# Dividing the eight PSUM banks of a recurrent mixer's loop anew: two pairs, one single bank, two for the attention

## The chip, the cores and the metric

The kernel runs on one core of one Trainium2 chip. The time is the device time of one execution in microseconds (us), from the hardware; lower is better. TensorE (PE) writes its matmul products to PSUM, which has eight banks; VectorE (DVE) and ScalarE (ACT) read them from there ("evict" them), GpSimd (POOL) works in SBUF, and SyncE (SP) issues most of the DMAs.

## The reference, cut to what matters

The program is two transformer blocks on a sequence of 1024 tokens with 1024 features. The second block mixes the tokens in two ways, and these two run together in the loop that is changed here:

```
y_fox  = fox_attention(q, k, v, log_f)                 # 8 heads of 64, causal, a decay as bias
for t in tokens:                                       # rwkv7_scan, 8 heads, state 64 x 64 a head
    sa = st @ a_t
    st = st * w_t + sa * b_t + v_t * k_t
    y_t = st @ r_t
merged = gate_fox * (y_fox @ w_o_fox) + gate_rwkv * (y_rwkv @ w_o_rwkv)
x      = x + merged @ w_out
```

The recurrent part ("rw" below) is computed in chunks: a triangular system is solved for each chunk of 64 tokens by doubling blocks, and only the state goes from chunk to chunk.

## The kernel before

The rw part is cut into eight units of 128 tokens (two chunks `c`, eight heads `h`). The function `b2` builds the loop. In each of its ten turns `together` interleaves three streams for every engine: `scan` of unit i-2, `inner` of unit i-1 and `pre` of unit i, and puts a piece of the attention ("fox", a `side` stream) between them. Each engine's order is fixed when the program is built, and an engine runs its instructions strictly in that order: a matmul that waits holds up everything behind it in PE's queue.

Every product takes a bank with `bk.take(key, ring)`. The ring is a tuple of bank numbers that are used in turn. The first matmul of the product waits until the bank's last product is evicted (`bk.room`, a semaphore `bank_emptied0` to `bank_emptied7`), its last matmul raises `bank_filled`, and DVE or ACT evict the bank and raise `bank_emptied`. A pair is named by its first bank and uses that bank's semaphores for both: pair 0 is banks 0 and 1.

These are the products of a unit, in PE's order around one turn of the loop, with the line of their matmuls and of the eviction:

- single products (`ONE_BANK`): `rw_n` (3596), `rw_b` (3601, evicted by DVE 3643), four turned operands `rw_turn` 0 to 3 (3608; 0 and 2 evicted by ACT 3697, 1 and 3 by DVE 3655), `rw_u` (3556, ACT 3872), `rw_k` 0 and 1 (3921 and 3922, DVE 3968), `rw_o` 0 and 1 (3931, DVE 3971), `rw_g` and `rw_kv` (both 3771, ACT 3862 and 3867), `rw_ot` (3940) and `rw_gate` (3950, DVE 3994);
- products of two banks (`PAIR`): `rw_mb` and `rw_qb` (both 3569, DVE 3823 and 3825, 3833 and 3834), `rw_t` (3758 and 3761, DVE 3839 and 3840), five times `rw_y` (3783, DVE 3845) and `rw_x` (3793 and 3797, DVE 3850 and 3854), `rw_w` (3812, ACT 3874), `rw_a` 0 and 1 (3906, DVE 3963 and 3964);
- the attention (`FB`): scores `fx_s` (3156), turned weights `fx_t` (3168), norms `fx_n` (3276), `fx_yt` (3288); its sums `fx_y` (3180) have bank 7 (`YB`).

The attention's first part runs earlier, between the matmuls of the gate projection (`a4`), which use banks 0 to 3. After the loop `pe_tail` begins the output projection: four tiles `o_tiles[:4]` of `w_o_fox` (lines 719 to 721, `pe_first_steps`) whose banks it is given as a ring. Then come a barrier and phase `a5`, whose first four tiles, of `w_o_rwkv`, take banks 0 to 3 of the common ring and wait for the room of all four before their first matmul. DVE evicts all these tiles at line 4115.

Of the kernel before, what the change touches and what calls it, by code (L numbers as in the profile page):

```python
# [218 lines left out]
def rest(n):  # L219
    for _ in range(n):  # L220
        yield
# [22 lines left out]
def program(nc, D, out, S):  # L244
# [3 lines left out]
    with ExitStack() as ctx:  # L248
        sigs = []

        def sem(name):
            return ctx.enter_context(nc.semaphore(name))
# [4 lines left out]
        def sig(name, step=1):  # L257
            n, of = over[step].pop() if over[step] else (0, sem(name))
            sigs.append(Sig(of, step))
            sigs[-1].n = sigs[-1].base = sigs[-1].covered = n  # L260
            return sigs[-1]
# [36 lines left out]
        def R(off, n, p0=0, p1=128):  # L298
            if off < H0:
                return XR[p0:p1, off:off + n]  # L300
            return BF[p0:p1, off - H0:off - H0 + n]
# [35 lines left out]
        bk = Banks(PS, [sem(f"bank_filled{b}") for b in range(8)], [sem(f"bank_emptied{b}") for b in range(8)])  # L337
# [10 lines left out]
        lhi, llo = sig("part_high"), sig("part_low")  # L348
# [37 lines left out]
        def nth(j):  # L386
            return sum(i not in by_blocks for i in range(j + 1))
# [4 lines left out]
        def wview(t, j):  # L392
            nk, n = order[j][2], order[j][4]
            return t[j % 2][:, 0:nk * n].rearrange("p (k c) -> p k c", k=nk)
# [309 lines left out]
        def pe_first_steps(e, tiles, x, ready, feats=None, side=None, at=None, ring=None):  # L704

            j, nk = tiles[0].j, tiles[0].nk
            wh, wl = wview(WH, j), wview(WL, j)
            ps = [bk.take(t.key, ring or RING) for t in tiles]
            e.wait_ge(s_wlo, nth(j))
            for t in tiles:  # L710
                e.wait_ge(*bk.room(t.key))
            for i, k in enumerate(feats or range(nk)):
                if i == at:
                    side(e)
                e.wait_ge(*ready(i))
                xh, xl = x(k)
                for n, t in enumerate(tiles):
                    sl, c = slice(t.hf * 512, t.hf * 512 + 512), slice(t.b, t.b + 128)
                    e.matmul(ps[n], wh[:, k, c], xh[:, sl], start=(i == 0), stop=False)  # L719
                    e.matmul(ps[n], wl[:, k, c], xh[:, sl], start=False, stop=False)  # L720
                    m = e.matmul(ps[n], wh[:, k, c], xl[:, sl], start=False, stop=(i == nk - 1))
                    if i == nk - 1:
                        m.then_inc(*bk.fill(t.key))
                yield
            wend[j] = bk.filled(tiles[-1].key)
# [2373 lines left out]
        def b2():  # L3099
# [4 lines left out]
                assert at_[0] <= F0 + 10 * T  # L3104
                return at_[0] - n

            PAIR, ONE_BANK, FB, YB = (0,), (2, 3), (4, 5, 6), (7,)
            QF, KF, VF, NCB = X0, X0 + T, X0 + 2 * T, [X0 + 3 * T, X0 + 4 * T]

            yo, free = R(F0 + 10 * T + 6, 512), F0 + 10 * T + 518  # L3110
# [319 lines left out]

            def pe_tail(e):
                yield from rest(TAIL + 2)
                yield from pe_first_steps(e, o_tiles[:4], hp, llo.at, None, None, None, (4, 5, 6, 7))

            def ve_tail(e):
                yield from rest(TAIL + 1)
# [37 lines left out]
            o_tiles = out_tiles()  # L3474
# [413 lines left out]
            def pe_scan(e, i):  # L3888
                u, w, rt, bb, kb, vT = (x[i % 2] for x in (us, wTs, rts, bbs, kbs, vTs))
                for b in range(2):  # L3890
                    h = (64 * b, 64 * b + 64)
                    key = ("rw_a", i, b)
                    bk.take(key, PAIR)
                    ps = bk.pair(key)
                    if b == 0:
                        e.wait_ge(*bk.emptied(("rw_w", i)))
                    if i + b == 0:
                        e.wait_ge(*rw_zero.at(0))
                    if i or b:
                        e.wait_ge(*bk.emptied(("rw_k", *divmod(2 * i + b - 1, 2))))  # L3900
                    e.wait_ge(*bk.room(key))
                    for at in (0, 256):
                        for q in range(4):
                            for g in range(2):
                                s_ = (64, 64 * g, 64 * g + 64)
                                m = e.matmul(ps[h[0]:h[1], g, at + 64 * q:at + 64 * q + 64],
                                             R(rt + q * 128 + 64 * b, *s_) if at else R(w + 256 * b + 64 * q, *s_),
                                             SR[64 * g:64 * g + 64, 64 * q:64 * q + 64], start=True, stop=True)
                    m.then_inc(*bk.fill(key))
                    yield  # L3910
                    key = ("rw_k", i, b)
                    ps = bk.take(key, ONE_BANK)
                    if b == 0:
                        for n in (2, 3):
                            e.wait_ge(*bk.emptied(("rw_turn", i, n)))
                    e.wait_ge(*rw_sub.at(2 * i + b))
                    e.wait_ge(*bk.room(key))
                    for q in range(4):
                        for g in range(2):
                            o, s_ = ps[64 * g:64 * g + 64, 64 * q:64 * q + 64], (64, *h)  # L3920
                            e.matmul(o, R(kb + (2 * q + g) * 64, *s_), R(vT + (2 * q + g) * 64, *s_), start=True, stop=False)
                            m = e.matmul(o, R(bb + (2 * q + g) * 64, *s_), R(u + (4 * g + q) * 64, *s_), start=False, stop=True)
                    m.then_inc(*bk.fill(key))
                    key = ("rw_o", i, b)
                    ps = bk.take(key, ONE_BANK)
                    if b == 0:
                        e.wait_ge(*bk.emptied(("rw_qb", i)))
                    e.wait_ge(*bk.room(key))
                    for q in range(4):
                        for g in range(2):  # L3930
                            m = e.matmul(ps[h[0]:h[1], (2 * q + g) * 64:(2 * q + g) * 64 + 64],
                                         R(qbs[i % 2] + (4 * g + q) * 64, 64, *h), R(u + (4 * g + q) * 64, 64, *h), start=True, stop=True)
                    m.then_inc(*bk.fill(key))
                    yield
# [130 lines left out]
        def out_tiles():  # L4065
            tiles = []
            for f in range(0, 8, 2):
                js = [wtile(n, 0, 4, f * 128, 256) for n in ("w_o_fox_2", "w_o_rwkv_2")]
                for s, j in enumerate(js):
                    for ff in range(2):  # L4070
                        for hf in range(2):
                            tiles.append(Tile(("o", s, f + ff, hf), j, 4, ff * 128, 128, 512, f + ff, hf, s,
                                              ff + hf == 0, ff + hf == 2))
            return tiles

        o_tiles = b2()
# [357 lines left out]
```

## Time and profile before

| | |
|---|---|
| time, median of 3 runs | 4202.17 us (4191.96 to 4206.91) |
| time of the profiled execution | 4194.41 us, span 4193.1 us |
| the recurrent loop | from about 2611 to 3150 us of the span |
| PE busy in 2631 to 3145 us | 403.85 of 514 us, granted clock 0.80 |
| DVE, ACT, POOL busy there | 283.30, 171.05, 124.87 us |

Most of the 4193 us are dense matmul phases outside the loop. In the loop no engine is always busy. "Granted clock" is the share of TensorE's full speed that the chip gave.

### The profile page before, as it was taken

The page shows a single profiled execution, that of the slowest core. Times are in us where ns is not written, and L with a number is a line of the kernel's source. Part 1 is how long each engine was busy: PE and PEld are TensorE (multiplying, and loading weights), DVE is VectorE, ACT ScalarE, POOL GpSimd, SP SyncE. Part 2 cuts the span into 40 slices and gives each one's busy share as a digit, 9 for nine tenths or more (in the row PEclk, how much of TensorE's full clock was granted, in tenths as well). Part 3 has the DMA queues.
Part 4 walks back from the last instruction along what each step waited for, and adds up shares of the span by engine and source line. Part 5 has one row for each costly group of instructions (what it writes and reads, how often), then busy time and mean ns, then how long its engine had stood idle before and what let it go on. Part 6 is the DMA issues. An engine that isn't in the chain of part 4 may idle for free. (4 is left out here: it accounts for less than half of the span.)

```text
span 4193.1 us, 75887 instructions
## 1 busy us (share of the span) xinstructions
PE 3875.4 (92%) x33370; PEld 3177.0 (76%) x33370; DVE 2251.9 (54%) x3662; ACT 1196.0 (29%) x1700; POOL 446.9 (11%) x440
## 2 busy tenths in 40 slices
PE   6999969888999999999999898788878999999999
PEld 5888847777867888888798576566667888888877
DVE  4643335555434666666624333555644476676673
ACT  5221234433223433121400323323323311111132
POOL 0001103231000442000000001222212000000000
PEclk9999979997999999999999899877879999999999
DMA  5211120113112334322322422111004211111111
GB/s 182 84 59 48 63 96 6 33 33 135 41 72 80 101 118 159 129 97 83 111 86 96 135 74 79 56 36 46 22 29 163 91 50 41 51 51 41 51 46 66
DMA packets 228061, 318.71 MB, mean 76 GB/s; under 512 B 17149, under 2 KB 172541, under 8 KB 227605
## 3 DMA queue, kind: packets, MB, share of 16 engines
q1 hardware_dynamic: 199088, 251.13, 18.1%
q10 hardware_dynamic: 28644, 62.72, 3.9%
q8 instruction: 265, 4.34, 0.4%
q14 instruction: 64, 0.52, 0.0%
HBM read 235.46 MB, written 78.35 MB: 75 GB/s over the span
## 5 line engine op out<-in xcount | busy, mean ns | idle before, releaser
L469 PE MATMUL ps<-sb_a_h,sb_whi 128*128 128x512 f32 (+1 forms) x2336 | 932.0, 399 | 6.2 <-DVE sb_wlo L430 5.7
L471 PE MATMUL ps<-sb_a_h,sb_whi 128*128 128x512 f32 (+1 forms) x2336 | 914.9, 392 | 0.0
L470 PE MATMUL ps<-sb_a_h,sb_wlo 128*128 128x512 f32 (+1 forms) x2336 | 914.8, 392 | 0.0
L469 PEld LDWEIGHTS ps<-sb_a_h,sb_whi 128*128 128x128 f32 (+1 forms) x2336 | 441.3, 189 | 116.6 <-issue 16.1
L470 PEld LDWEIGHTS ps<-sb_a_h,sb_wlo 128*128 128x128 f32 (+1 forms) x2336 | 441.6, 189 | 95.0 <-issue 5.2
L471 PEld LDWEIGHTS ps<-sb_a_h,sb_whi 128*128 128x128 f32 (+1 forms) x2336 | 440.9, 189 | 94.9
L420 ACT ACTIVATE sb_whi<-sb_wraw 128x2048 fp32r<-128x2048 f32 (+3 forms) x132 | 233.7, 1771 | 810.4 <-PE ps L471 494.5
L675 DVE TENSOR_TENSOR sb_x<-sb_x,ps 128x512 f32<-128x512 f32 x480 | 314.7, 683 | 211.5 <-PE ps L471 197.1
L430 DVE TENSOR_TENSOR sb_wlo<-sb_wraw,sb_whi 128x2048 fp32r<-128x2048 f32 (+3 forms) x132 | 281.9, 2135 | 224.6 <-ACT sb_whi L420 203.9
L469 PE MATMUL ps<-sb_a_g,sb_whi 128*128 128x512 f32 x896 | 349.8, 390 | 11.5 <-DVE sb_x L675 10.5
L471 PE MATMUL ps<-sb_a_g,sb_whi 128*128 128x512 f32 x896 | 348.7, 389 | 0.0
L470 PE MATMUL ps<-sb_a_g,sb_wlo 128*128 128x512 f32 x896 | 348.6, 389 | 0.0
L469 PEld LDWEIGHTS ps<-sb_a_g,sb_whi 128*128 128x128 f32 x896 | 168.2, 188 | 50.6 <-DVE sb_x L675 14.7
L471 PEld LDWEIGHTS ps<-sb_a_g,sb_whi 128*128 128x128 f32 x896 | 168.2, 188 | 35.1
L470 PEld LDWEIGHTS ps<-sb_a_g,sb_wlo 128*128 128x128 f32 x896 | 168.2, 188 | 34.6
L4230 DVE TENSOR_TENSOR sb_a_f<-ps,sb_root 128x512 f32<-128x512 f32 x88 | 60.9, 692 | 101.9 <-PE ps L471 96.2
L3249 POOL TENSOR_TENSOR sb_b<-sb_x,sb_consts 128x128 f32<-128x128 f32 x64 | 30.1, 485 | 611.0 <-DMA sb_x<-fox_c 399.2
L4280 ACT ACTIVATE sb_a_g<-sb_a_f 128x512 fp32r<-128x512 f32 x44 | 27.8, 633 | 226.0 <-DVE sb_a_f L4250 226.0
L526 PE MATMUL ps<-sb_a_h,sb_whi_blocks 128*128 128x512 f32 x224 | 87.2, 389 | 0.0
L527 PE MATMUL ps<-sb_a_h,sb_wlo_blocks 128*128 128x512 f32 x224 | 87.2, 389 | 0.0
L528 PE MATMUL ps<-sb_a_h,sb_whi_blocks 128*128 128x512 f32 x224 | 87.2, 389 | 0.0
L719 PE MATMUL ps<-sb_a_h,sb_whi 128*128 128x512 f32 x128 | 56.5, 442 | 25.0 <-DVE sb_wlo L430 8.5
(589 smaller groups left out, 6657.9 us busy)
## 6 DMA issues: line engine op xcount, KB each, us to landing
sb_wraw<-w_in SPq DMA_DIRECT2D x33, 1024.0 KB, 5.2
sb_wraw<-w_ff SPq DMA_DIRECT2D x32, 1024.0 KB, 5.4
sb_wraw<-w_up SPq DMA_DIRECT2D x22, 1024.0 KB, 5.1
sb_wraw<-w_down SPq DMA_DIRECT2D x11, 1024.0 KB, 4.9
sb_wraw<-w_xkv SPq DMA_DIRECT2D x8, 1024.0 KB, 5.5
sb_wraw<-w_out SPq DMA_DIRECT2D x8, 1024.0 KB, 5.3
sb_b<-rw_d SPq DMA_DIRECT2D x16, 512.0 KB, 6.4
sb_b<-y SPq DMA_DIRECT2D x16, 512.0 KB, 5.8
```

The costliest lines, as they stand in the source:

```text
L420: e.activation(WH[j % 2][:, 0:m], WR[j % 2][:, 0:m], ACT.Copy).then_inc(s_whi, 1)
L430: e.tensor_tensor(WL[j % 2][:, 0:m], WR[j % 2][:, 0:m], WH[j % 2][:, 0:m].bitcast(F32), ALU.subtract).then_inc(s_wlo, 1)
L469: e.matmul(o, wh[:, k, c], xh[:, sl], start=(k == 0), stop=False)
L470: e.matmul(o, wl[:, k, c], xh[:, sl], start=False, stop=False)
L471: m = e.matmul(o, wh[:, k, c], xl[:, sl], start=False, stop=(k == t.nk - 1))
L526: e.matmul(o, wh[:, k, :], xhi, start=(opens and k == 0), stop=False, skip_group_check=True)
L527: e.matmul(o, wl[:, k, :], xhi, start=False, stop=False, skip_group_check=True)
L528: m = e.matmul(o, wh[:, k, :], xlo, start=False, stop=(k == 3), skip_group_check=True)
L675: e.tensor_tensor(o, o, bk[t.key], ALU.add).then_inc(*bk.empty(t.key))
L719: e.matmul(ps[n], wh[:, k, c], xh[:, sl], start=(i == 0), stop=False)
L3249: e.tensor_tensor(nms[g], R(NCB[g] + qb * 128, 128), C("causal"), ALU.subtract).then_inc(*fx_nm[g].up())
L4230: e.tensor_tensor(raw[:, 2:514], bk[t.key], RR[:, span(t.hf)], ALU.mult).then_inc(*bk.empty(t.key))
```

## The change

The change deals the eight banks of `b2` out anew. Pair products get two pairs in turn, 0 and 1 or 2 and 3, except the last unit's two `rw_a`, which use only pair 0. Single products, which had banks 2 and 3 in turn, have bank 4 alone. The attention has banks 5 and 6 where it had 4, 5 and 6, in the part between the gate matmuls too. The four tiles of `pe_tail` use banks 2, 3, 5 and 6 where they used 4 to 7.

```diff
@@ -3104,7 +3104,7 @@
-            PAIR, ONE_BANK, FB, YB = (0,), (2, 3), (4, 5, 6), (7,)
+            PAIR, LAST_PAIR, ONE_BANK, FB, YB = (0, 2), (0,), (4,), (5, 6), (7,)
@@ -3430,7 +3430,7 @@
             def pe_tail(e):
                 yield from rest(TAIL + 2)
-                yield from pe_first_steps(e, o_tiles[:4], hp, llo.at, None, None, None, (4, 5, 6, 7))
+                yield from pe_first_steps(e, o_tiles[:4], hp, llo.at, None, None, None, (2, 3, 5, 6))
@@ -3890,7 +3890,7 @@
                 for b in range(2):
                     h = (64 * b, 64 * b + 64)
                     key = ("rw_a", i, b)
-                    bk.take(key, PAIR)
+                    bk.take(key, PAIR if i < 7 else LAST_PAIR)
                     ps = bk.pair(key)
```

No instruction is added, removed or moved on any engine; only addresses in PSUM and what is waited for change. On PE, where `rw_turn` 0 and 1 of unit 1, the last `rw_x` of unit 0, `rw_turn` 2 and 3 of unit 1 and `rw_u` of unit 0 follow each other, before:

```order
L3608 MATMUL ps<-sb_consts,sb_b 128x128 [waits bank_emptied2,rw_al]
...
L3608 MATMUL ps<-sb_consts,sb_b 128x128 [waits bank_emptied3,gd_in1]
...
L3793 MATMUL ps<-sb_b 64x32 [waits bank_emptied0]
...
L3608 MATMUL ps<-sb_consts,sb_b 128x128 [waits bank_emptied2,rw_k_end]
...
L3608 MATMUL ps<-sb_consts,sb_b 128x128 [waits bank_emptied3,rw_b_end]
...
L3556 MATMUL ps<-sb_b 64x64 [waits bank_emptied2,bank_emptied0]
```

and after:

```order
L3608 MATMUL ps<-sb_consts,sb_b 128x128 [waits bank_emptied4,rw_al]
...
L3608 MATMUL ps<-sb_consts,sb_b 128x128 [waits bank_emptied4,gd_in1]
...
L3793 MATMUL ps<-sb_b 64x32 [waits bank_emptied0,bank_emptied2]
...
L3608 MATMUL ps<-sb_consts,sb_b 128x128 [waits bank_emptied4,rw_k_end]
...
L3608 MATMUL ps<-sb_consts,sb_b 128x128 [waits bank_emptied4,rw_b_end]
...
L3556 MATMUL ps<-sb_b 64x64 [waits bank_emptied4,bank_emptied0]
```

Each of the four turned operands and `rw_u` now wait for the eviction of the single product just ahead of them; before they waited for the one before that.

On PE a little later, where `rw_mb` of unit 1 follows the first `rw_a` of unit 0, and then `rw_k`, `rw_o`, `rw_qb`, the second `rw_a`, `rw_t`, `rw_g`, `rw_k`, `rw_o` and `rw_kv`, before:

```order
L3569 MATMUL ps<-sb_b 64x64 [waits rw_kt,bank_emptied0,rw_bt,rw_al]
...
L3921 MATMUL ps<-sb_b 64x64 [waits rw_u_more,bank_emptied3,bank_emptied2]
...
L3931 MATMUL ps<-sb_b 64x64 [waits bank_emptied2,bank_emptied0]
...
L3569 MATMUL ps<-sb_b 64x64 [waits bank_emptied0,rw_rt]
...
L3906 MATMUL ps<-sb_b 64x64 [waits bank_emptied0,bank_emptied3]
...
L3758 MATMUL ps<-sb_consts,sb_b 64x64 [waits bank_emptied0,rw_x0]
...
L3771 MATMUL ps<-sb_b 64x64 [waits bank_emptied3,bank_emptied0]
...
L3921 MATMUL ps<-sb_b 64x64 [waits bank_emptied2,rw_u_more]
...
L3931 MATMUL ps<-sb_b 64x64 [waits bank_emptied3]
...
L3771 MATMUL ps<-sb_b 64x64 [waits bank_emptied2,bank_emptied3,bank_emptied0]
```

and after:

```order
L3569 MATMUL ps<-sb_b 64x64 [waits rw_kt,bank_emptied2,rw_bt,rw_al]
...
L3921 MATMUL ps<-sb_b 64x64 [waits rw_u_more,bank_emptied4]
...
L3931 MATMUL ps<-sb_b 64x64 [waits bank_emptied4,bank_emptied2]
...
L3569 MATMUL ps<-sb_b 64x64 [waits bank_emptied0,rw_rt]
...
L3906 MATMUL ps<-sb_b 64x64 [waits bank_emptied2,bank_emptied4]
...
L3758 MATMUL ps<-sb_consts,sb_b 64x64 [waits bank_emptied0,rw_x0]
...
L3771 MATMUL ps<-sb_b 64x64 [waits bank_emptied4,bank_emptied2]
...
L3921 MATMUL ps<-sb_b 64x64 [waits bank_emptied4,rw_u_more]
...
L3931 MATMUL ps<-sb_b 64x64 [waits bank_emptied4]
...
L3771 MATMUL ps<-sb_b 64x64 [waits bank_emptied4,bank_emptied0]
```

The pairs alternate, so `rw_mb`, `rw_qb`, the second `rw_a` and `rw_t` each wait for the pair product before the last. The six single products here each wait for the one just ahead.

At the end of the loop, the first matmul of `pe_tail` on PE, before and after:

```order
L719 MATMUL ps<-sb_a_h,sb_whi_57 128x512 [waits bank_emptied6,bank_emptied7,bank_emptied5,part_low,bank_emptied4,weights_low_part]
```

```order
L719 MATMUL ps<-sb_a_h,sb_whi_57 128x512 [waits bank_emptied5,bank_emptied6,bank_emptied3,part_low,bank_emptied2,weights_low_part]
```

and the first matmul of phase `a5` behind the barrier, which reads the same in both:

```order
L719 MATMUL ps<-sb_a_h,sb_whi_56 128x512 [waits barrier_Pool_Activation_PE_DVE_SP_release,bank_emptied2,bank_emptied3,bank_emptied1,part_low,bank_emptied0,weights_low_part]
```

The last products in banks 2 and 3 were `rw_ot` and `rw_gate` of unit 7 before; after the change they are the first two tiles of `pe_tail`.

## Rows read from the trace of the kernel before

**Rows 1.** Page, part 1: busy us (share of the span) and instructions

```profile
PE 3875.4 (92%) x33370; PEld 3177.0 (76%) x33370; DVE 2251.9 (54%) x3662; ACT 1196.0 (29%) x1700; POOL 446.9 (11%) x440
```

**Rows 2.** Busy time by stretch: before the loop, the loop, behind it

```profile
core 0: us, PE busy (x) PEld busy (x) DVE busy (x) ACT busy (x) POOL busy (x), PEclk, DMA share, GB/s
...
2631.00:3145.00 514.00, 403.85 (x8190) 334.44 (x8189) 283.30 (x627) 171.05 (x282) 124.87 (x128) 0.80 0.13 39
2350.00:2610.00 260.00, 240.40 (x1174) 185.67 (x1173) 83.06 (x217) 74.33 (x114) 14.71 (x32) 0.98 0.25 83
...
3181.00:3243.00 62.00, 62.00 (x275) 51.38 (x274) 25.35 (x30) 19.24 (x30) 17.07 (x13) 1.00 0.49 168
```

**Rows 3.** Waits, 2631 to 3145 us: who for whom, total, times, longest

```profile
PE ps L3783 <- DVE sb_b L3854: 16.9, 14, 2.5
...
PE ps L3569 <- DVE sb_b L3964: 10.1, 7, 1.7
...
PE ps L3168 <- ACT sb_x L3232: 9.1, 9, 2.3
...
PE ps L3906 <- DVE sb_b L3834: 8.9, 6, 1.8
PE ps L3758 <- DVE sb_b L3964: 8.4, 7, 1.5
PE ps L3556 <- ACT sb_b L3697: 4.4, 4, 1.9
```

**Rows 4.** Groups, 2631 to 3145 us: busy, mean ns, idle before and releasers

```profile
L3569 PE MATMUL ps<-sb_b 64*64 64x64 f32 x1024 | 21.3, 233 | 12.2 <-DVE sb_b L3964 10.1 <-DVE sb_b L3825 1.5 <-issue 0.6
```

**Rows 5.** Timeline of PE, 2674 to 2701 us: start, us, what, idle before

```profile
2675.64 1.09 PE L3608 MATMUL ps<-sb_consts,sb_b 128*128 128x128 f32 x8
2676.66 0.67 PE L3793 MATMUL ps<-sb_b 64*64 64x32 f32 x32
2677.26 1.09 PE L3608 MATMUL ps<-sb_consts,sb_b 128*128 128x128 f32 x8
...
2679.01 1.08 PE L3556 MATMUL ps<-sb_b 64*64 64x64 f32 x29
...
2681.45 1.15 PE L3906 MATMUL ps<-sb_b 64*64 64x64 f32 x32 [0.82 <-ACT sb_b L3874]
2684.15 1.16 PE L3569 MATMUL ps<-sb_b 64*64 64x64 f32 x64 [1.56 <-DVE sb_b L3964]
...
2686.05 1.03 PE L3931 MATMUL ps<-sb_b 64*64 64x64 f32 x15
2686.89 0.28 PE L3569 MATMUL ps<-sb_b 64*64 64x64 f32 x3
...
2693.57 1.65 PE L3758 MATMUL ps<-sb_consts,sb_b 64*64 64x64 f32 x26 [1.48 <-DVE sb_b L3964]
```

**Rows 6.** Timeline of DVE, 2674 to 2701 us

```profile
2686.05 0.68 DVE L3825 TENSOR_TENSOR sb_b<-ps,sb_consts 128x512 f32<-128x512 f32 x1
...
2687.25 0.42 DVE L3968 TENSOR_TENSOR sb_b<-sb_b,ps 128x256 f32<-128x256 f32 x1
...
2698.24 0.42 DVE L3968 TENSOR_TENSOR sb_b<-sb_b,ps 128x256 f32<-128x256 f32 x1 [1.13 <-PE ps L3922]
2699.24 0.69 DVE L3971 TENSOR_TENSOR sb_b<-sb_b,ps 64x512 f32<-64x512 f32 x1 [0.58 <-PE ps L3931]
```

**Rows 7.** Evictions of single products by line: ns min/median/max

```profile
L3697 ACT ACTIVATE sb_b<-ps x16: 575/597/599, 2628.2 to 3068.1; 128x512 f32<-128x512 f32 x16
...
L3655 DVE COPY sb_b<-ps x16: 678/692/693, 2630.1 to 3068.5; 128x512 f32<-128x512 f32 x16
```

**Rows 8.** Behind the loop, 3140 to 3185 us: timelines of PE and DVE

```profile
3166.90 0.79 PE L719 MATMUL ps<-sb_a_h,sb_whi 128*128 128x512 f32 x1 [8.51 <-DVE sb_wlo L430]
...
3165.62 1.22 DVE L430 TENSOR_TENSOR sb_wlo<-sb_wraw,sb_whi 128x1024 fp32r<-128x1024 f32 x1
...
3169.27 2.48 DVE L4115 TENSOR_TENSOR sb_x<-sb_a_f,ps 128x512 f32<-128x512 f32 x4 [0.15 <-ACT sb_a_f L4141]
```

## Prediction

> **What bounds the kernel now.** I read the page first. PE is busy in 92% of the span and no other engine in much over half [rows 1], so a change counts by what it does to PE's queue. The stretches then show where PE is not saturated. Between the gate matmuls PE is busy 240 of 260 us at clock 0.98, behind the loop all 62 of 62 us, but in the recurrent loop only 404 of 514 us, while DVE is busy 283 [rows 2]. So 110 us of the loop are waits of PE, and the loop is a chain that goes to and fro: PE fills a bank, DVE or ACT evicts it, and PE, which runs strictly in order, waits. Third, the waits of this stretch by releaser [rows 3]. The reader is to sort them into waits for data and waits for a bank. `rw_y` waiting for `rw_x`'s eviction (16.9 us) is data and stays. `rw_mb` waiting for the eviction of `rw_a` (10.1 us, 7 times), the second `rw_a` for that of `rw_qb` (8.9, 6 times) and `rw_t` for that of the second `rw_a` (8.4, 7 times) are waits for pair 0 alone: the waiting product does not read what was evicted. One more, 1.5 us, is `rw_qb` behind `rw_mb` in unit 0 [rows 4]. Together 28.9 us. Last, one turn of the loop on PE and on DVE [rows 5, 6], from which the hand-offs are priced.
>
> **What the second pair gives.** The pairs alternate, so the four waits go. But DVE is in order too, and takes part back.
>
> - `rw_mb`: its 1.56 us of idle [rows 5] end, seven times, 10.1 us. Behind it stand `rw_k` and `rw_o`, which now share a bank. `rw_o` started at 2686.05 on the other single bank. It must now wait for DVE 3968, which ended at 2687.67, since DVE first evicts `rw_mb` (3823, 3825) and makes one step more [rows 5, 6]: 1.7 to 1.8 us late against the old order, 1.77 with the hand-off. In three of the seven turns attention matmuls stand there and DVE is free, and the wait is the overlap of two products, 0.2, the eviction, 0.42, and both hand-offs, 0.2: 0.8. So 4 x 1.77 + 3 x 0.8 = 9.5 us come back: near nothing is gained here.
> - The second `rw_a` and `rw_t`: 8.9 + 8.4 + 1.5 = 18.8 us of idle go. `rw_t` now waits for `rw_qb`, whose two evictions (2 x 0.68) and hand-offs (0.2) outlast the one `rw_a` that PE has in between (1.15) by 0.35: 7 x 0.35 = 2.4 us back. Gain 16.4.
>
> The hand-offs are the 1.56 us idle of `rw_mb` less two evictions of 0.68: 0.2 for both ways.
>
> **What the one single bank costs.** Two banks let PE fill one while the other is evicted. With one, each adjacent single product costs the overlap, the eviction and 0.2.
>
> - The turned operands: four a unit, and two follow in about 1.02 us, one each 0.5 (from 2675.64 to 2676.66) [rows 5]. One after another, each takes its own 0.6, an eviction of 0.60 by ACT or 0.69 by DVE [rows 7], and 0.2: 1.4 to 1.5 us. So `rw_turn` 1 comes 0.95 late. `rw_x` and its 0.6 us stand ahead of `rw_turn` 2, which comes 0.4 later still; `rw_turn` 3 again 0.95, and `rw_u`, behind 1.25 us already, 0.3 to 0.4. That is 2.6 us a unit and 21 over eight. In four units `rw_u` waited for ACT's eviction already, 4.4 us [rows 3], which covers part: I take 19. Queued behind are `rw_u`, `rw_w` and the first `rw_a`, the path itself, so nothing hides it.
> - `rw_g`, `rw_k`, `rw_o`, `rw_kv` in one row: three hand-offs, each an overlap of 0.2 to 0.3 (`rw_o`, 1.03 from 2686.05, and the next product from 2686.89 [rows 5]), evictions of 0.60, 0.42 and 0.69 [rows 6, 7], and 0.2: 1.1 + 0.9 + 1.2 = 3.2 us. Seven turns would be 22; where attention matmuls stand between, part is covered: 19.
> - `rw_gate` behind `rw_b`: 0.2 + 0.69 + 0.2 = 1.1 us in six units. What follows on DVE is often late anyway: 3.5 in all.
> - The attention with two banks: in the loop only where four score or weight products follow each other, 1.5 us. Between the gate matmuls nothing: at least nine of those, some 2 us, part the pieces, longer than any of the evictions there, and PE stays full [rows 2]. If that cover were gone each piece would cost 0.5 us, about 15 in all; I see no cause.
> - In unit 7, `rw_o` twice behind `rw_k`: 0.85 each, 1.7 us, on the chain to the last output.
>
> **Behind the loop.** Phase `a5` starts its first four tiles at 3166.90, released by the weights [rows 8]. They need banks 0 to 3, all four before the first matmul. Now banks 2 and 3 hold the first two tiles of `pe_tail`, which DVE evicts from 3169.27, four in 2.48 us: the second is done at about 3170.5. The group starts at 3170.7, 3.8 us late, and the phase behind it is dense [rows 2], so the 3.8 us stay.
>
> **The sum.** Gains 10.1 + 18.8 = 28.9. Costs 9.5 + 2.4 + 19 + 19 + 3.5 + 1.5 + 1.7 + 3.8 = 60.4. That is 31.5 us slower. I take off 4, because PE waits nine times for ACT's exponentials, 9.1 us [rows 3], and some of these do not move with PE: +28. The profiled execution took 4194.4 us; by this it would take 4222. It lies 7.8 below the median of the three runs, which themselves spread by 15, so I put +28 on the median: **4230 us**.
>
> **The bounds.** High: no cover anywhere, 21 + 22 for the two rows of singles, 7 x 1.77 = 12.4 for `rw_o`, 6.6 for the gates, 6 for the attention, 2.4 + 1.7 + 3.8 behind: 76 less 28.9, +47, 4249. Low: half of the loop's costs of single banks and of the attention, 52.5, are hidden, the rest stands: 26 + 2.4 + 1.7 + 3.8 - 28.9 = +5, 4207.
>
> **A rule to weigh.** PE's gaps of 1.5 us recur in every unit and end when a bank is emptied [rows 3, 5]. The Trainium skill (Perfetto Trace Analysis, Optimization Strategy) says that the same gap repeated on an engine that should be saturated can mean that too little PSUM is left for the next tile. By that reading the second pair is the cure and the sum is its 28.9 us of gain, which is the faster rival below. The same page (Optimizing Tensor Performance, Matmuls) wants independent matmul groups to rotate through different banks, so that an eviction overlaps the next group. That is what the single products lose here, and it speaks against this change. The rows price the two sides at 28.9 and some 55 us; the page prices neither.
>
> **The rivals.**
>
> - *The delays are hidden* (0.16). DVE ends some evictions late for other reasons, and PE idles 110 us in the loop; if half of the single products' delay falls into waits that come anyway, the change is +5 to +12 us: about 4212, between no change and a little slower. Against it: the rows of single products end in `rw_u` and in `rw_y`, which have no wait of their own worth more than 0.2 us in the plain turn.
> - *Faster* (0.07). The pair waits are the loop's true bound and the single products run ahead of it. It decides if less than 20 of the loop's 55 us of delays stand; with 10, the sum is 10 + 8 - 28.9 = -11, 4191. For it: these waits are the longest for a bank. Against it: PE is in order, and no single product of those rows has slack in front of the next pair product.
> - *More than the sum* (0.15). Every hand-off stands, and more idle pieces lower the clock: the loop's mean is 0.80 already [rows 2]. 4% more on 404 us of matmuls is 16 us: 4245 to 4255.
> - *The second pair gives nothing*, because DVE evicts in order anyway, is a part of the last two: the 16.4 us of `rw_a` and `rw_t` would be lost too, and +28 would be +44, 4246.
>
> **Chances.** The forecast, +13 to +40, has 0.62. Slower by over 0.3% (12.6 us, about what a measurement of this kernel tells from no change) takes 0.62, 0.15 and a quarter of the hidden case, 0.04: 0.81. Within 0.3%: 0.12. Faster: 0.07. The range 4207 to 4249 joins the two bounds and leaves out some 2 in 10.
>
> **What would show it.** In the trace of after, PE 3569, 3906 and 3758 wait for DVE 3964 and 3834 no more, or only 3758 for 3834 with 0.3 us each. In their place stand waits of PE 3608 for ACT 3697 and DVE 3655, some 0.9 us each and three a unit, of PE 3931 for DVE 3968, of PE 3921 for ACT 3862, of PE 3771 for DVE 3971. The loop from the first `rw_mb` to the last `rw_o`, 514 us now, takes about 536. PE 719 behind the barrier waits for DVE 4115 instead of DVE 430. Up to 2610 us nothing moves. I am wrong if the waits of 3608 and 3771 are there and the loop is not longer, or if the part before the loop stretches.

## The result, and the profile after

The changed kernel takes 4251.65 us, median of 4 executions (4244.3 to 4268.48); the kernel before, measured beside it, 4203.68 us. The ratio is 1.0132, with a 95% interval of 1.01 to 1.0164: 1.3% slower. I had forecast 4230 us and a range up to 4249. The direction was right, the size 20 us short, and the result lies 2.65 us outside the range.

The profiled execution took 4251.71 us, its span is 4250.3 us against 4193.1. The page of after, part 1 (busy us, share of the span, instructions) and the row of the granted clock in 40 slices of part 2:

```profile
PE 3919.3 (92%) x33370; PEld 3201.4 (75%) x33370; DVE 2254.8 (53%) x3662; ACT 1196.6 (28%) x1700; POOL 445.6 (10%) x440
...
PEclk8999979998999999999999898787778999999999
```

The loop lies in slices 25 to 31, which read 8787778. PE executes the same 33370 instructions as in [rows 1], but is busy for 43.9 us more. DVE, ACT and POOL are within 3 us of before. That is the first sign of something that the forecast's sum does not hold: it is a sum of waits.

The stretches of after (us, busy time by engine, then granted clock, DMA share, GB/s). The loop runs here from the first `rw_mb` to the last `rw_ot`:

```profile
core 0: us, PE busy (x) PEld busy (x) DVE busy (x) ACT busy (x) POOL busy (x), PEclk, DMA share, GB/s
2635.42:3201.49 566.07, 445.43 (x8195) 360.32 (x8195) 286.19 (x621) 175.02 (x286) 123.92 (x126) 0.74 0.12 35
2350.00:2610.00 260.00, 241.35 (x1174) 186.35 (x1172) 83.52 (x218) 73.54 (x111) 12.95 (x30) 0.98 0.25 83
3240.00:3302.00 62.00, 62.00 (x275) 51.35 (x274) 24.68 (x29) 17.83 (x27) 16.36 (x13) 1.00 0.49 166
```

And the same loop of the kernel before, with the same two ends:

```profile
2631.51:3148.71 517.20, 407.05 (x8195) 336.94 (x8195) 284.53 (x625) 174.39 (x287) 124.80 (x128) 0.80 0.13 38
```

Read them as a ledger. The loop grew by 48.9 us. PE's idle time in it went from 517.20 - 407.05 = 110.15 to 566.07 - 445.43 = 120.64, only 10.5 more. The other 38.4 are busy time, mostly longer matmuls, and the granted clock goes with them: 0.80 before, 0.74 after. The two other stretches are as in [rows 2]. Of the span's 57.2 us, the rest is 3.9 up to the first `rw_mb`, and 4.4 behind the last `rw_ot`. Two hand-offs of 0.8 us, of the first unit's turned operands, lie in the 3.9; the rest of it is not told from chance, since the first `rw_mb` starts anywhere from 2626.2 to 2636.9 us in the traces of this document. The forecast had 22 us more for the loop, 514 to about 536.

The waits of PE in after from 2633 to 3202 us (who for whom, total us, times, longest), those that the change moved. One of the 15 in the first row, 0.8 us, lies just ahead of the first `rw_mb`:

```profile
PE ps L3608 <- ACT sb_b L3697: 15.8, 15, 2.7
PE ps L3783 <- DVE sb_b L3854: 13.7, 12, 3.0
PE ps L3931 <- DVE sb_b L3968: 13.0, 16, 1.8
...
PE ps L3793 <- DVE sb_b L3845: 7.3, 7, 1.6
PE ps L3950 <- DVE sb_b L3643: 7.1, 5, 2.8
...
PE ps L3771 <- DVE sb_b L3971: 6.0, 7, 0.9
...
PE ps L3556 <- DVE sb_b L3655: 4.3, 5, 0.9
...
PE ps L3921 <- ACT sb_b L3862: 3.5, 6, 0.8
...
PE ps L3758 <- DVE sb_b L3834: 1.6, 3, 0.8
PE ps L3608 <- DVE sb_b L3655: 1.3, 4, 0.3
```

Two rows of the same view of before, which answer to some of them and were not among [rows 3]:

```profile
PE ps L3793 <- DVE sb_b L3845: 12.0, 10, 1.9
...
PE ps L3608 <- ACT sb_b L3697: 1.6, 1, 1.6
```

The four pair waits of [rows 3, 4] are gone, 28.9 us. The hand-offs stand in their place: 15.5 more ahead of the turned operands (L3608), 13.0 ahead of `rw_o` (L3931), 7.1 ahead of `rw_gate` (L3950), 6.0 ahead of `rw_kv` (L3771), 3.5 ahead of `rw_k` (L3921), 1.6 ahead of `rw_t` (L3758), and `rw_u` (L3556) waits 4.3 as it waited 4.4. That is 46.6 of new waits against 28.9. And the two data waits of the chain, of `rw_y` and `rw_x` (L3783, L3793), shrank by 3.2 and 4.7. Why is not shown. That DVE catches up while PE waits elsewhere would explain it, but they shrink by 3.8 and 2.5 in the kernel mix below too, where PE has no hand-offs to wait in. 46.6 - 28.9 - 7.9 = 9.8, which is near the 10.5 of the ledger; the rest are smaller rows.

The timeline of PE in after for the turn of [rows 5] (start, us, what, idle before and its releaser):

```profile
2680.97 0.66 PE L3608 MATMUL ps<-sb_consts,sb_b 128*128 128x128 f32 x4
2682.40 0.63 PE L3608 MATMUL ps<-sb_consts,sb_b 128*128 128x128 f32 x4 [0.78 <-ACT sb_b L3697]
2682.96 0.67 PE L3793 MATMUL ps<-sb_b 64*64 64x32 f32 x32
2683.91 0.63 PE L3608 MATMUL ps<-sb_consts,sb_b 128*128 128x128 f32 x4 [0.28 <-DVE sb_b L3655]
2685.31 0.99 PE L3608 MATMUL ps<-sb_consts,sb_b 128*128 128x128 f32 x4 [0.78 <-ACT sb_b L3697]
...
2691.23 1.10 PE L3569 MATMUL ps<-sb_b 64*64 64x64 f32 x62
...
2695.09 1.35 PE L3931 MATMUL ps<-sb_b 64*64 64x64 f32 x15 [1.35 <-DVE sb_b L3968]
...
2696.30 1.85 PE L3569 MATMUL ps<-sb_b 64*64 64x64 f32 x60
...
2709.70 1.83 PE L3771 MATMUL ps<-sb_b 64*64 64x64 f32 x29 [0.94 <-DVE sb_b L3971]
```

The turned operands now come 1.43 and 1.40 us apart where the forecast had 1.4 to 1.5. `rw_mb` at 2691.23 follows at once. And here the clock can be seen. The fourth turned operand takes 0.99 us where the three ahead of it take 0.63 to 0.66: the granted clock falls from 1.00 to 0.86 in 2684 to 2686 and is 0.50 in 2686 to 2688, where in before it stays 1.00 up to 2692. A little later `rw_qb` at 2696.30 takes 1.85 us for 60 matmuls of the form of which `rw_mb` does 62 in 1.10. It ran at 1.2 GHz (granted clock 0.50 from 2696 to 2698), behind the 1.35 us in which PE stood ahead of `rw_o`. In before both products ran at 2.4 GHz (1.00 from 2684 to 2688). Over the whole loop the trace has the lower level for 205 us in 18 stretches before, and for 290 us in 27 stretches after.

Behind the loop, PE's and DVE's timelines of after:

```profile
3224.96 0.77 PE L719 MATMUL ps<-sb_a_h,sb_whi 128*128 128x512 f32 x1 [12.65 <-DVE sb_x L4115]
```

```profile
3223.42 2.48 DVE L4115 TENSOR_TENSOR sb_x<-sb_a_f,ps 128x512 f32<-128x512 f32 x4 [0.15 <-ACT sb_a_f L4141]
```

The first tile of `a5` waits for L4115 instead of L430, 12.65 us against 8.51 in [rows 8], as forecast.

### The profile page after: what moved, and what is told of

Read it like the earlier page. It is cut to its first block and busy times, and to the rows that moved or that the text cites. A ratio compares the mean times of both kernels' runs of the same rounds, so it can differ in the third digit from the quotient of the medians.

```text
span 4250.3 us, 75887 instructions
## 1 busy us (share of the span) xinstructions
PE 3919.3 (92%) x33370; PEld 3201.4 (75%) x33370; DVE 2254.8 (53%) x3662; ACT 1196.6 (28%) x1700; POOL 445.6 (10%) x440
## 3 DMA queue, kind: packets, MB, share of 16 engines
q1 hardware_dynamic: 199088, 251.13, 17.8%
## 5 line engine op out<-in xcount | busy, mean ns | idle before, releaser
L430 DVE TENSOR_TENSOR sb_wlo<-sb_wraw,sb_whi 128x2048 fp32r<-128x2048 f32 (+3 forms) x132 | 281.9, 2136 | 223.8 <-ACT sb_whi L420 203.1
L469 PE MATMUL ps<-sb_a_g,sb_whi 128*128 128x512 f32 x896 | 349.8, 390 | 11.5 <-DVE sb_x L675 10.5
L526 PE MATMUL ps<-sb_a_h,sb_whi_blocks 128*128 128x512 f32 x224 | 87.2, 389 | 0.0
```

The lines of the kernel that those rows point to most:

```text
L430: e.tensor_tensor(WL[j % 2][:, 0:m], WR[j % 2][:, 0:m], WH[j % 2][:, 0:m].bitcast(F32), ALU.subtract).then_inc(s_wlo, 1)
L469: e.matmul(o, wh[:, k, c], xh[:, sl], start=(k == 0), stop=False)
L526: e.matmul(o, wh[:, k, :], xhi, start=(opens and k == 0), stop=False, skip_group_check=True)
```

## The experiments

**The theories.** *C*: the hand-offs cost little more than their waits, but the new idle pieces make TensorE's granted clock fall in the loop, and the matmuls run longer. *W*: the hand-offs themselves (or the attention's two banks) are the whole loss, and the clock of that one execution is chance. Each ratio below is to the kernel before on the same chip. Two changed kernels that are compared below have not always run on the same chip. A row under an experiment is the loop of its profiled execution alone, from the first `rw_mb` to the last `rw_ot`, in the columns above.

**One single bank alone.**

```diff
-            PAIR, ONE_BANK, FB, YB = (0,), (2, 3), (4, 5, 6), (7,)
+            PAIR, ONE_BANK, FB, YB = (0,), (2,), (4, 5, 6), (7,)
```

> The kernel before with one bank for single products (bank 2) in place of two; one pair, three attention banks and the start of phase a5 as before. Theory C (the clock): each hand-off that I priced comes, and the new short idle pieces make the granted clock of the loop fall below its 0.80, as in the trace of after (0.75). The gaps ahead of the single products grow by about 45 us as they did in after, some 8 are absorbed elsewhere, and PE's busy time in the loop rises by 25 to 40: 62 to 80 us slower than before, loop clock 0.73 to 0.77. Rival W (waits alone; the 20 us missing from my sum are hand-offs or attention waits, the clock is chance): the clock stays 0.79 to 0.81, PE busy within 8 us of 404, and the time is 35 to 50 us longer.

Measured: 4280.96 us, ratio 1.0204 (1.0186 to 1.0222), 84 us slower than before's 4196.99.

```profile
2628.21:3239.01 610.80, 474.33 (x8195) 384.52 (x8195) 287.67 (x621) 174.98 (x286) 123.93 (x126) 0.70 0.11 33
```

Idle time is 136.5, 26 us over before; PE's busy time is 67 us over it, at clock 0.70. W's 35 to 50 us are far off. C named the mechanism, but both its parts came out otherwise: fewer waits (26, not 37) and a lower clock (0.70, not 0.73 to 0.77) with more busy time (67, not 25 to 40), and the total is 4 us over its range.

**Two banks for the attention alone.**

```diff
-            PAIR, ONE_BANK, FB, YB = (0,), (2, 3), (4, 5, 6), (7,)
+            PAIR, ONE_BANK, FB, YB = (0,), (2, 3), (5, 6), (7,)
```

> The kernel before with two banks (5, 6) in place of three for the attention, nothing else changed (bank 4 lies idle). My sum has 1.5 us for it: the time within 5 us of before, clock of the loop 0.79 to 0.81. Rival A (the missing 20 us are the attention's): 10 us or more slower, with new waits of PE 3156, 3168, 3276 or 3288 for evictions of the attention's banks.

Measured: 4201.1 us, ratio 1.0005 (0.999 to 1.002): nothing.

```profile
2630.14:3151.96 521.82, 414.72 (x8195) 341.96 (x8195) 285.30 (x621) 174.94 (x287) 124.27 (x127) 0.80 0.13 38
```

The third bank of the attention was worth nothing that can be measured here (0.1% either way is 4 us). The missing 20 us are not here.

**The hand-offs taken away, the pairs kept** (*mix*). Two pairs as in after. Every second single product takes the first bank of the next pair:

```diff
-                    ps = bk.take(("rw_turn", i, n), ONE_BANK)
+                    ps = bk.take(("rw_turn", i, n), PAIR if n % 2 else ONE_BANK)
...
-                    ps = bk.take((name, i), ONE_BANK)
+                    ps = bk.take((name, i), PAIR if name == "rw_kv" else ONE_BANK)
...
                     key = ("rw_k", i, b)
-                    ps = bk.take(key, ONE_BANK)
+                    ps = bk.take(key, PAIR if i < 7 else LAST_ONE)
...
-                ps = bk.take(("rw_gate", i), ONE_BANK)
+                ps = bk.take(("rw_gate", i), PAIR if i < 7 else LAST_ONE)
```

`LAST_ONE` is (2, 3), for `rw_o` and `rw_ot` of unit 7 too, and `pe_tail` takes banks 4 to 7 again.

> Two pairs as in after, but rw_k, rw_kv, rw_turn 1 and 3 and rw_gate take the next pair's first bank, so that no two neighbouring single products share a bank; the last unit and the start of a5 use the banks of before. Theory C: the pair waits go (24 to 28 us as measured in after: 9.9 + 7.8 + 6.8 + 1.5), no hand-off comes, and with fewer idle pieces the loop's clock is 0.80 or higher: 25 to 45 us faster than before, 4160 to 4180. Rival P (two pairs by themselves lower the clock or cost time, whatever the single products do): clock of the loop near 0.75 again, PE busy some 35 us over before, and the time 0 to 15 us over before.

Measured: 4170.74 us, ratio 0.9946 (0.9928 to 0.9963), 26 us faster than before by the medians and 23 by the ratio.

```profile
2629.86:3118.43 488.57, 401.37 (x8196) 329.88 (x8196) 284.30 (x621) 174.99 (x287) 124.26 (x127) 0.80 0.14 41
```

The timeline of PE in mix at the places of [rows 5]:

```profile
2673.55 1.09 PE L3608 MATMUL ps<-sb_consts,sb_b 128*128 128x128 f32 x8
2674.57 0.67 PE L3793 MATMUL ps<-sb_b 64*64 64x32 f32 x32
2675.16 1.09 PE L3608 MATMUL ps<-sb_consts,sb_b 128*128 128x128 f32 x8
...
2682.93 1.03 PE L3931 MATMUL ps<-sb_b 64*64 64x64 f32 x15
```

The turned operands again follow each other two by two, and `rw_o` starts with no wait. Waits of PE in the loop of mix, of `rw_y`, `rw_x` and `fx_t` (before: 16.9, 12.0, and for `fx_t` 9.1 and 3.5):

```profile
PE ps L3783 <- DVE sb_b L3854: 13.1, 12, 2.4
PE ps L3168 <- ACT sb_x L3232: 11.2, 13, 2.4
PE ps L3793 <- DVE sb_b L3845: 9.5, 8, 1.8
PE ps L3168 <- ACT sb_b L3232: 6.7, 3, 2.9
```

Idle time falls by 23 us to 87.2: this is the gain of the second pair without the price of the single products (I had put it at 28.9). Two pairs by themselves do not lower the clock. C's time was 25 to 45 us faster; 26 by the medians is at its lower end, 23 by the ratio just below it. Its clock, 0.80 or higher, came as 0.80: less idle time did not raise it.

**The hand-offs kept, their idle time filled** (*padded*). The kernel after, with matmuls of the identity with itself ahead of the bank waits, into the pair that is free. They are overwritten unread. They wait until that pair is evicted; the kernel's own products and waits are all there.

```diff
+            def pe_pad(e, n):
+                b = PAIR[bk.spot.get(PAIR, 0) % 2]
+                e.wait_ge(bk.free[b], bk.turn[b])
+                for _ in range(n):
+                    e.matmul(bk.ps[:, b, 0:128], C("ident"), C("ident"), start=True, stop=True)
...
+                    if n % 2:
+                        pe_pad(e, 5)
                     e.wait_ge(*bk.room(("rw_turn", i, n)))
```

In the same way 4 ahead of `rw_kv`, 6 and 3 ahead of the two `rw_o`, 5 ahead of `rw_gate`.

> The kernel after, with 3 to 6 extra 128x128 products of the identity with itself ahead of the bank waits of rw_turn 1 and 3, rw_o, rw_kv and rw_gate, into the pair that is free; their results are overwritten unread. The waits stay, but PE is busy in them. Theory C: the idle pieces made the clock fall, so it comes back to 0.80 or more in the loop, and the kernel is 20 to 45 us faster than after (4205 to 4232). Theory W (the hand-offs themselves take the 48 us): the clock has no part in it, the extra products are hidden or cost up to 10 us, and the time is 4250 to 4262.

Measured: 4225.95 us, ratio 1.0067 (1.0051 to 1.0084). After's interval begins at 1.01, so more work made the kernel faster, by about 27 us.

```profile
2632.44:3178.15 545.71, 447.06 (x8585) 373.61 (x8585) 285.32 (x621) 174.43 (x286) 123.94 (x126) 0.85 0.12 37
```

The group of the extra products (x390 records, two to a matmul; busy us), and PE's timeline at the first of them:

```profile
L3555 PE MATMUL ps<-sb_consts 128*128 128x128 f32 x390 | 58.0, 300 | 0.0
```

```profile
2678.34 0.66 PE L3616 MATMUL ps<-sb_consts,sb_b 128*128 128x128 f32 x4
2678.84 1.28 PE L3555 MATMUL ps<-sb_consts 128*128 128x128 f32 x10
2679.95 0.60 PE L3616 MATMUL ps<-sb_consts,sb_b 128*128 128x128 f32 x4
```

`rw_turn` 1 starts 1.61 us after `rw_turn` 0, a little later than in after (1.43): the hand-off is still there and costs no less. What changed is that PE worked in it. The clock rose to 0.85, the loop lost 20.4 us, and the kernel's own products take some 389 us (447.06 - 58.0) where they took 445. W's 4250 to 4262 is excluded. So is chance in one execution: the mean clock of the whole span was 0.947 to 0.954 in all six executions of padded, 0.930 to 0.937 in the four of after and 0.941 to 0.951 in those of before.

**Half of the turned operands' hand-offs taken away.**

```diff
-                    ps = bk.take(("rw_turn", i, n), ONE_BANK)
+                    ps = bk.take(("rw_turn", i, n), PAIR if n % 2 else ONE_BANK)
```

> The kernel after, with rw_turn 1 and 3 alone put into the next pair's first bank, so that the hand-offs among the four turned operands go and all others stay. In the trace of after the gaps ahead of rw_turn 1 and 3 are 15 us in all. Theory C (the clock amplifies each hand-off): 22 to 35 us faster than after, the loop's clock 0.76 to 0.79. Theory W (a hand-off costs its wait): 12 to 17 us faster, clock within 0.01 of after's 0.74.

Measured: 4227.32 us, ratio 1.007 (1.0047 to 1.0093), 24 us below after, or 26 by the ratios.

```profile
2626.21:3165.86 539.65, 425.73 (x8195) 344.96 (x8195) 285.55 (x621) 174.51 (x287) 124.18 (x127) 0.78 0.12 37
```

The loop is 26.4 us shorter than after's. The idle time fell by 6.7 to 113.9, PE's busy time by 19.7. Some 3 of these are overlap that two neighbouring products have again (0.2 each, 15 times); the rest, more than half of what these hand-offs cost, was clock. The time agrees with C, but by itself it is a weak witness against W's 12 to 17 us: the two intervals leave some 16 us either way on the 26. A closer one is the next kernel, run on the same chip, with the waits of after in the loop: all its six executions are slower than all six of this one, by 22 us in the medians, although it has 4 to 5 us less behind the loop. This trace is of the fastest of the six executions.

**The tail's banks.**

```diff
-                ps = bk.take(("rw_ot", i), ONE_BANK)
+                ps = bk.take(("rw_ot", i), ONE_BANK if i < 7 else LAST_ONE)
...
-                yield from pe_first_steps(e, o_tiles[:4], hp, llo.at, None, None, None, (2, 3, 5, 6))
+                yield from pe_first_steps(e, o_tiles[:4], hp, llo.at, None, None, None, (4, 5, 6, 7))
```

`rw_gate` takes its bank as `rw_ot` does.

> The kernel after, with the first four tiles of pe_tail in banks 4 to 7 as before, and the last unit's rw_ot and rw_gate in banks 2 and 3. Both theories: the start of phase a5 comes 3.5 us earlier against rw_gate 7, and that gate loses its 1.4 us wait, so the profiled time is about 5 us below after's 4251.7 but for chance, and PE 719 waits for DVE 430 again. Nothing in the loop up to rw_ot 7 moves.

Measured: 4249.29 us, ratio 1.0121 (1.0096 to 1.0146), which time alone does not tell from after. The trace does, in PE's timeline at the start of `a5` and in the loop's row:

```profile
3238.30 0.79 PE L719 MATMUL ps<-sb_a_h,sb_whi 128*128 128x512 f32 x1 [8.62 <-DVE sb_wlo L430]
```

```profile
2636.87:3219.98 583.11, 462.77 (x8196) 372.77 (x8196) 286.60 (x621) 174.72 (x286) 123.98 (x126) 0.72 0.11 34
```

The wait is 8.62 us and for L430 again, against 12.65, and the last `rw_gate` starts without the 0.87 us that it waited in after. From the last `rw_ot` to the start of `a5` it is 18.3 us against 23.5: the 5 us that were expected. The loop holds a surprise. Its code is that of after up to the last unit's end, and its idle time is 120.34 us, after's to 0.3. But it took 17.0 us longer, all of it in longer matmuls, at clock 0.72. So nothing in the loop was to move, and in these two traces the waits repeat while the clock does not.

**Can the clock be bought?** The kernel mix, with matmuls of the identity in the bank that the next product will overwrite, in the places where PE idled over some 0.5 us in its trace. The numbers of matmuls are a table by product; 386 in the first kernel. For them the wait for the bank's room comes ahead of the wait for the data:

```diff
+            PADS = {
+                ('fx_t', 1, 6, 0, 0): 13, ('rw_x', 0, 0): 4, ('rw_y', 0, 2): 5, ('fx_t', 1, 7, 0, 0): 10, ('rw_y', 0, 3): 14,
...
+            def pe_pad(e, key, ps):
+                if key in PADS:
+                    e.wait_ge(*bk.room(key))
+                    for _ in range(PADS[key]):
+                        e.matmul(ps[:, 0:128], C("ident"), C("ident"), start=True, stop=True)
```

> The kernel mix with 386 extra 128x128 products of the identity, in 45 places where PE idled over 0.5 us in mix's trace, each group a little shorter than the idle time, in the bank that the next product will overwrite. Theory C (the clock of the loop is lost to idle pieces): clock 0.88 or more, the products fill 30 us or more faster, 20 to 45 us faster than mix (4125 to 4150). Rival (the clock is not what bounds mix; the chain of evictions is): the waits grow by what the products shrink, and the time is 0 to 10 us from mix's 4171.

Measured: 4175.35 us, ratio 0.995 (0.9933 to 0.9966): the time of mix. The loop, and the group of the extra products:

```profile
2630.09:3129.63 499.54, 445.64 (x8967) 383.70 (x8967) 285.67 (x621) 174.99 (x287) 124.54 (x127) 0.93 0.13 40
```

```profile
L3124 PE MATMUL ps<-sb_consts 128*128 128x128 f32 x772 | 99.4, 284 | 10.2 <-ACT sb_b L3721 4.7 <-DVE sb_b L3859 1.5 <-ACT sb_x L3259 1.4
```

The clock came, 0.93, and the kernel's own products took 346 us instead of 401. But C's 4125 to 4150 did not come; the rival's time did, 0 to 10 us from mix's. I had reckoned each extra product too short: it takes 257 ns (99.4 us for 386), and 99.4 us of them do not fit into 87 us of idle time. So the next two kernels have 159 and 85 of them, in nearly the same places with smaller numbers. The first line of the table with 386 and with 159:

```diff
-                ('fx_t', 1, 6, 0, 0): 13, ('rw_x', 0, 0): 4, ('rw_y', 0, 2): 5, ('fx_t', 1, 7, 0, 0): 10, ('rw_y', 0, 3): 14,
+                ('fx_t', 1, 6, 0, 0): 5, ('rw_x', 0, 0): 2, ('rw_y', 0, 2): 2, ('fx_t', 1, 7, 0, 0): 5, ('fx_t', 1, 7, 1, 0): 1,
```

> The kernel mix with 159 of the extra products in place of 386, in the same places. In mix_padded the real products took 55 us less than in mix (445.6 - 99.4 = 346 against 401) at clock 0.93, but the extra ones lasted 257 ns each, 99.4 us where the idle time had been 75, and pushed the path. 159 of them are some 41 us, inside the idle time. Theory C: the clock is 0.85 to 0.90, the loop 20 to 35 us shorter than mix's 489, the time 4135 to 4155. Rival (what the clock gives, the chain of evictions takes as waits): within 6 us of mix's 4171.

> The kernel mix with 85 extra products, about 22 us, in the longest idle pieces first. Theory C with a threshold of activity: the clock is 0.80 to 0.87 and the time between mix_light's and mix's. Rival: within 6 us of mix.

Measured: 4155.6 us, ratio 0.9902 (0.988 to 0.9925), with 159, and 4153.27 us, ratio 0.9897 (0.9875 to 0.992), with 85. Their loops:

```profile
2634.23:3110.72 476.49, 405.40 (x8514) 338.34 (x8514) 285.21 (x621) 174.65 (x287) 124.09 (x127) 0.92 0.14 42
```

```profile
2626.72:3106.84 480.12, 401.38 (x8365) 332.45 (x8365) 284.71 (x621) 174.78 (x287) 124.19 (x127) 0.88 0.14 41
```

Their groups of extra products (busy us behind the bar):

```profile
L3125 PE MATMUL ps<-sb_consts 128*128 128x128 f32 x318 | 51.3, 306 | 10.3 <-ACT sb_b L3722 5.2 <-DVE sb_b L3860 1.4 <-ACT sb_x L3260 1.4
L3124 PE MATMUL ps<-sb_consts 128*128 128x128 f32 x170 | 32.1, 317 | 9.0 <-ACT sb_b L3721 5.1 <-ACT sb_x L3259 1.4 <-DVE sb_b L3859 1.4
```

Both are faster than before and than mix, at 0.990 of before's time, and their intervals lie below that of mix, though not by much. The loops are 12.1 and 8.5 us shorter than mix's; I had expected 20 to 35 for the first. The clocks are 0.02 and 0.01 over their ranges, and the second time was to lie between the first and mix's. Clocks of 0.92 and 0.88 give less than they seem to. The extra products take 51.3 and 32.1 us, more than the 41 and 22 reckoned. The kernel's own take 47 and 32 us less than mix's, yet the loops lose only 12.1 and 8.5: three quarters of what the clock gives goes into further waits, and into extra products that fill or outlast them. In padded it was 56 us of products for 20.4 of loop. So the rival's mechanism holds for most of it, though its time, within 6 us of mix's, does not. The two kernels cannot be told apart in time.

All runs together. Loop, busy, idle and clock are of the profiled execution, whose time stands beside the median (idle is the loop less PE's busy time; the extra products count as busy). The last column is the mean clock of the whole span, lowest and highest of all executions:

| kernel | median us | ratio to before | profiled us | loop us | PE busy | idle | clock | clock, whole span |
|---|---|---|---|---|---|---|---|---|
| before | 4203.68 | 1 | 4194.41 | 517.2 | 407.1 | 110.2 | 0.80 | 0.941 to 0.951 |
| after | 4251.65 | 1.0132 | 4251.71 | 566.1 | 445.4 | 120.6 | 0.74 | 0.930 to 0.937 |
| one single bank | 4280.96 | 1.0204 | 4285.86 | 610.8 | 474.3 | 136.5 | 0.70 | 0.930 to 0.934 |
| attention with two | 4201.1 | 1.0005 | 4196.26 | 521.8 | 414.7 | 107.1 | 0.80 | 0.942 to 0.951 |
| turns apart | 4227.32 | 1.007 | 4216.08 | 539.7 | 425.7 | 113.9 | 0.78 | 0.936 to 0.942 |
| tail back | 4249.29 | 1.0121 | 4266.03 | 583.1 | 462.8 | 120.3 | 0.72 | 0.931 to 0.939 |
| padded | 4225.95 | 1.0067 | 4227.29 | 545.7 | 447.1 | 98.7 | 0.85 | 0.947 to 0.954 |
| mix | 4170.74 | 0.9946 | 4164.67 | 488.6 | 401.4 | 87.2 | 0.80 | 0.944 to 0.948 |
| mix, 386 extra | 4175.35 | 0.995 | 4175.54 | 499.5 | 445.6 | 53.9 | 0.93 | 0.959 to 0.965 |
| mix, 159 extra | 4155.6 | 0.9902 | 4155.09 | 476.5 | 405.4 | 71.1 | 0.92 | 0.956 to 0.963 |
| mix, 85 extra | 4153.27 | 0.9897 | 4151.23 | 480.1 | 401.4 | 78.7 | 0.88 | 0.955 to 0.963 |

## Why the forecast was right in direction and short in size

- **The pair waits: right.** All four went, 28.9 us, and `rw_t` got 1.6 back where I said 2.4. My own terms make it 0.41 us a unit (1.36 + 0.2 - 1.15), not 0.35, which is 2.9. Alone, with no hand-off beside them, the pairs are worth 23 us of idle time (mix). There the attention's `fx_t` waits 7.0 us longer for ACT (12.6 to 19.6, two small rows with it), which takes back a part; `rw_y` and `rw_x` wait 6.3 less.
- **`rw_o` behind `rw_k`: near.** I had 9.5 for the first of a unit, some 5.4 for the second (its share of the 19) and 1.7 in unit 7, 16.6 with the lost overlap; its waits are 13.0 us, 16 in number, which with 0.2 of overlap each makes 16.2. In the plain turn the wait is 1.35, for 1.77 in all.
- **The turned operands: right.** 15.4 us of waits with `rw_u`, for a term of 19 that also held the lost overlap: two operands took 1.09 us together [rows 5] and now take 0.66 and 0.63.
- **`rw_g`, `rw_k`, `rw_o`, `rw_kv`: too dear.** `rw_k` waits 3.5 in six units and `rw_kv` 6.0 in seven, where 1.1 and 1.2 a turn had been priced; the longest waits, 0.8 and 0.9, are near the price less the overlap, but `rw_k` meets the full one in four units only.
- **`rw_gate`: too cheap.** 7.1 us in five units and 0.87 in unit 7, for 3.5. I had called part of it hidden, on the grounds that DVE is late anyway. It was not: three waits are 0.88, and two, 1.74 and 2.77, are longer than the hand-off of 1.1.
- **The attention: right.** 1.5 forecast; the run with two banks alone shows no change.
- **The start of `a5`: right.** 3.8 forecast; the wait grew from 8.51 to 12.65 (4.1) and shrank to 8.62 when the banks went back.
- **Cover: too small.** I took off 4 us for waits that come anyway. The data waits of `rw_y` and `rw_x` alone shrank by 7.9. The nine waits for ACT's exponentials, which I had given as the reason, did not: 9.1 before, 9.4 after.

So the sum of waits was too high: 23.7 for the loop (27.7 less the 4), against 10.5 of idle time. The forecast's terms hold the lost overlap too. With some 33 more breaks between products, at 0.2 each, that is an estimated 7 us more, 17 in all, and the sum was some 6 too high.

**The step that failed** is that the sum held no term for the clock. It stood among the rivals (*more than the sum*), with 4% of 404 us, 16 us, and a chance of 0.15. It measured more. At 0.80 the lower level holds for 40% of 517 us, at 0.74 for 52% of 566: 87 us more at 1.2 GHz (the traces have 85). With PE busy for 0.79 of it and products that take some 1.7 times as long (1.10 to 1.85 us above), that is an estimated 28 us, most of the 38.4 by which PE's busy time grew; the 7 of lost overlap are most of the rest. That the idle pieces of the hand-offs lower the clock is shown by padded (same waits, filled: clock 0.85), and turns apart (two hand-offs a unit fewer: 0.78) and, in the other direction, one single bank alone (0.70) agree. The two errors had opposite signs: too much for the waits, nothing for the clock. By the estimate this change would have come out near +20 without the clock; padded, at 0.85 but with its extra products to run, is at +28. That the result, 4251.65, lies in the 4245 to 4255 of that rival is in part luck, since it had every hand-off at its full price and 16 us of clock.

The other rivals: the delays were not half hidden, since 46.6 us of new waits stand; the change was not faster, although mix shows that the gain of the second pair is real once nothing pays for it; and the second pair did give something.

The rule that I weighed against this change held. The Trainium skill (Perfetto Trace Analysis, Optimizing Tensor Performance, Matmuls) wants independent groups to rotate through different banks, and rotating them is most of what turned +48 us into -26 us in mix (some 5 of the 74 are the banks of the tail). So did the other one, that equal bubbles can mean too little PSUM (the same page, Optimization Strategy): the 23 us were there.

**What stays open.** The share of idle time does not set the clock: it is 21.3% in before and in after, at 0.80 and 0.74, and 17.8% in mix, at 0.80 again. What about the place or the length of the idle pieces decides was not settled, nor why 23 us less of them left the clock of mix where it was. And the loop figures come from one trace a kernel, while two traces of nearly the same loop differ by 17 us.

## What to carry to other kernels

Weigh a new wait of PE twice in a stretch whose clock is already below 1: once for itself, and once for what it may do to the matmuls around it. Here 10 us of net waits came with some 30 us of slower matmuls. It does not hold backwards: 23 us of idle time taken away in mix brought no faster clock. When banks are short, give neighbouring products different banks before giving any product a pool of its own; a small product may well use one bank of a free pair. And where PE must wait anyway, throw-away matmuls a little shorter than the wait can pay a little, as many as fit: in mix 85 of them took 8.5 us off the loop and 386 added 11.0.

## What the hardware showed that I had not expected

- More work was faster: 195 extra matmuls in the waits, 58.0 us of them, made the loop 20.4 us shorter.
- The same loop code, with idle time equal to 0.3 us, took 566.1 us at clock 0.74 in one execution and 583.1 us at 0.72 in another. Over the six executions of the kernel with the tail's banks put back, the fastest, 4239.75 us, had a mean clock of 0.939 over the whole span and the slowest, 4266.03 us, 0.931. The clock goes with the times, but is not all of their spread: an execution of 4252.06 us has 0.931 too.
- The Trainium skill (TensorE: Matmul & The Clock Gate, A second HAM failure mode: psum-queue depth-cycling) tells of a kernel in which short idle times of PE between groups, as it goes through the banks, make the clock go up and down. These traces agree that the clock goes up and down (between 1.00 and 0.50 in the turn above), and the loss stands in the matmuls themselves: 1.85 us against 1.10 for nearly the same number.
